# A two-layer fp32 block on one core: the opening loads and norms x first, and the context's rows are turned and normed beside the third and fourth query panel

## The reference, cut to what matters

```python
mod   = silu(c) @ ada_w + ada_b            # 1024 x 6144; shift1, scale1 are its first 2048 columns
mod_c = silu(c_ctx) @ ada_w + ada_b
h  = modulate(rms_norm(x,   norm1_w), sh1,  sc1)
hc = modulate(rms_norm(ctx, norm1_w), sh1c, sc1c)
q = h @ w_in[:, 0:512]                      # q is wanted for x alone
k, v, dt, xbc                               # are wanted for x and for the context
```

## Time and profile before

| | |
|---|---|
| runs | 2733.73, 2733.86, 2742.72 us; median 2733.86 |
| span of the profiled execution | 2732.2 us, which lies 1.7 us under the median |
| PE busy | 2546.3 us, 93% of the span |
| DVE, ACT, POOL busy | 50%, 36%, 36% |
| first and last product of query panels 0 and 1 | about 34 and 59 us |
| query panel 2 and 3 | from 61.17 and 67.31 us |
| first key panel | from 73.85 us |

### The profile page before, as it was taken

The page is one execution under the profiler, slowest core; times in us unless marked ns, Lnnn a source line. Parts: engine busy times, 40 slices in busy tenths (PEclk is TensorE's granted clock), DMA queues, the critical chain, the costliest instruction groups (busy, mean ns, idle before and its releaser), DMA issues.

```text
span 2732.2 us, 45723 instructions
## 1 busy us (share of the span) xinstructions
PE 2546.3 (93%) x19794; PEld 2286.5 (84%) x19794; DVE 1369.3 (50%) x2057; ACT 973.2 (36%) x1565; POOL 985.7 (36%) x585
## 2 busy tenths in 40 slices
PE   7989978799999999999999999989998979999997
PEld 5877767678888888887999999988988968999997
DVE  4634455462635354444264554466654534727363
ACT  5234344232323444334433332354332224333232
POOL 1743344544444322222434444500002214445444
PEclk9999999999999999999999999999999988999998
DMA  9432120333332221111222332322111012233221
GB/s 248 121 94 63 53 70 24 92 96 97 93 93 87 68 55 47 40 47 40 78 62 85 89 90 85 87 59 70 40 33 36 17 32 59 85 92 87 87 87 60
DMA packets 379927, 201.33 MB, mean 74 GB/s; under 512 B 6464, under 2 KB 377152, under 8 KB 379728
## 3 DMA queue, kind: packets, MB, share of 16 engines
q1 hardware_dynamic: 379728, 198.42, 25.8%
HBM read 196.30 MB, written 2.10 MB: 73 GB/s over the span
## 4 chain that ended last, share of the span: by engine, by line
PE 57%; DVE 22%; ACT 11%; issue 4%; POOL 4%; DMA 1%; POOLq 0%; ACTq 0%; SPq 0%; DVEq 0%
PE ps L645 40%; DVE t_ffy L2829 7%; ACT t_wh L613 5%; DVE t_ffy L2832 2%; ACT t_ffy L2736 2%; DVE t_atq L2628 2%; POOL t_wl L623 1%; PE ps L2436 1%; DVE t_wl L623 1%; DVE t_ffy L2838 1%; PE ps L3061 1%; PE ps L2409 1%; PE ps L2375 1%; PE ps L3080 1%; PE ps L1090 1%
## 5 line engine op out<-in xcount | busy, mean ns | idle before, releaser
L623 POOL TENSOR_TENSOR t_wl<-t_raw,t_wh 128x1024 fp32r<-128x1024 f32 (+2 forms) x268 | 611.1, 2281 | 1030.1 <-ACT t_wh L613 1030.1
L613 ACT ACTIVATE t_wh<-t_raw 128x1024 fp32r<-128x1024 f32 (+2 forms) x323 | 327.7, 1015 | 605.8 <-PE ps L645 562.4
L645 PE MATMUL ps<-t_hh,t_wh 128*128 128x264 f32 (+2 forms) x2048 | 473.4, 310 | 14.4 <-DVE t_dcq L2562 3.6
L645 PE MATMUL ps<-t_hh,t_wl 128*128 128x264 f32 (+2 forms) x2048 | 449.4, 298 | 8.0 <-POOL t_wl L623 4.3
L645 PE MATMUL ps<-t_hl,t_wh 128*128 128x264 f32 (+2 forms) x2048 | 446.0, 299 | 0.0
L645 PEld LDWEIGHTS ps<-t_hh,t_wh 128*128 128x128 f32 x2048 | 323.7, 192 | 36.5 <-issue 17.6
L645 PEld LDWEIGHTS ps<-t_hh,t_wl 128*128 128x128 f32 x2048 | 324.0, 191 | 24.2 <-POOL t_wl L623 6.9
L645 PEld LDWEIGHTS ps<-t_hl,t_wh 128*128 128x128 f32 x2048 | 322.6, 191 | 9.1 <-issue 1.5
L645 PE MATMUL ps<-t_fhh,t_wh 128*128 128x264 f32 (+1 forms) x1040 | 280.9, 324 | 6.5 <-DVE t_fhl L1753 4.9
L645 PE MATMUL ps<-t_fhh,t_wl 128*128 128x264 f32 (+1 forms) x1040 | 281.5, 325 | 4.6 <-POOL t_wl L623 4.5
L2829 DVE SCALAR_TENSOR_TENSOR t_ffy<-t_ffp,t_vec,t_ffy 128x528 f32<-128x528 f32 x88 | 216.8, 2463 | 130.6 <-ACT t_ffy L2736 130.6
(11 more groups left out here) (558 smaller groups left out, 4351.3 us busy)
## 6 DMA issues: line engine op xcount, KB each, us to landing
t_raw<-in_up SPq DMA_DIRECT2D x44, 512.0 KB, 3.8
t_raw<-in_up2a SPq DMA_DIRECT2D x44, 512.0 KB, 3.9
t_raw<-in_up2b SPq DMA_DIRECT2D x44, 512.0 KB, 3.9
t_raw<-in_attn_in SPq DMA_DIRECT2D x33, 512.0 KB, 4.1
t_raw<-in_dn_in SPq DMA_DIRECT2D x33, 512.0 KB, 4.1
t_raw<-in_ada_w SPq DMA_DIRECT2D x32, 512.0 KB, 4.4
t_raw<-in_w_in SPq DMA_DIRECT2D x25, 512.0 KB, 4.4
t_raw<-in_down SPq DMA_DIRECT2D x16, 512.0 KB, 3.8
```

Of the source, the lines that this page charges most:

```text
L613: ac.activation(wh[slot_of[j]][:, 0:kc, :], raw[r % NRAW][:, 0:kc, :], ACT.Copy).then_inc(up("wh_cut", "cut", j), 1)
L623: eng.tensor_tensor(wl[slot_of[j]][:, 0:kc, :], raw[r % NRAW][:, 0:kc, :], wh[slot_of[j]][:, 0:kc, :].bitcast(F), SUB).then_inc(up(name, " ...
L645: ins = pe.matmul(ps[bank_of(j, i)][:, 0:tn], wt[slot][:, k, :], a[:, k, t0:t0 + tn], start=first, stop=last)
```

## The change

x's four tiles come first and then four `ada_w` panels instead of context, meta rows and three. Slots become 12, and the copies of x out of PSUM go to VectorE, the Squares stay on ScalarE. The dummy matmuls go. A Sqrt on a scratch value is put behind the Silu. The context's and the meta rows' loads stand behind the last `ada_w` panel in SP's queue. Their turns, in banks of the ring of four, and the roots of the context's norm come when query panel 2 is taken; its spread and the 8 `norm1` and 8 `low1` of the context come when query panel 3 is taken. The diff, cut to its core:

```diff
-                    w.wait_ge(s.squared, at("squared", "turn_x", 4 + r))
+                    w.wait_ge(s.squared, at("squared", "turn_x", 2 + r))
...
-        xin = [slot(qT, 0), slot(qT, 1), slot(kT, 2), slot(zs, 0), slot(zs, 1), slot(vT, 0), slot(vT, 1)]
-        room = [slot(vT, 2)] + [slot(xbc, i) for i in range(6)]
-        slots = room + xin
+        xin = [slot(qT, 0), slot(qT, 1), slot(kT, 2), slot(zs, 0), slot(vT, 0), slot(vT, 1), meta_in]
+        room = [slot(vT, 2)] + [slot(xbc, i) for i in range(6)] + [slot(zs, 1)]
+        slots = room + xin[0:4]
...
+        def put_turn(i, of):
+            put("turn_x", i, banks=2, of=of)
+            for h in range(2):
+                sig.mark(copied_by(i), "turn_x", i, str(h))     # scaled (DVE) for i < 4, else copied (ACT)
+            if i < 6:
+                sig.mark("squared", "turn_x", i)
...
-        for i in range(7):
-            put("turn_x", i, banks=2, of=8)
-            if i < 6:
-                sig.mark("squared", "turn_x", i)
+        for i in range(4):
+            put_turn(i, 8)
         load_to(1)
         put("ada_rest")
         put_roots(NORM_X)
-        put_roots(NORM_C)
         put("ada_mm", 0, banks=1)
         put("ada_mm", 1, banks=1)
-        put_busy(NORM_X, 0, 5)
         put("ada_set", 0, banks=1)
         put_spread(NORM_X)
-        put_spread(NORM_C)
...
             put("norm1", c, x) ...
-            if c:
-                put("low1", c - 1, "c")
-            norm1_of(c, "c")
             put("low1", c, "x")
...
-                for i, (src, n, _, _) in enumerate(comes):
-                    sp.dma_start(xin[i][0:n, :], src).then_inc(slot_in[7 + i], 16)
-                for i in range(3):
+                for i in range(4):
+                    come(i)
+                for i in range(4):
                     ada_panel(i)
...
             def ada_rest():
-                for i in range(3, 7):
+                for i in range(4, 8):
                     ada_panel(i)
-                for i in range(7):
-                    w.wait_ge(s.copied, at("copied", "turn_x", i, "1"))
-                    ada_panel(7 + i)
+                for i in range(4):
+                    w.wait_ge(s.squared, at("squared", "turn_x", i))
+                    w.wait_ge(s.scaled, at("scaled", "turn_x", i, "1"))
+                    ada_panel(8 + i)
             def ada_mm(i):
-                if i < 2:
+                if i < 4:
                     w.wait_ge(s.ada_mm, at("ada_mm", "ada_mm", i))
-                    ada_panel(14 + i)
+                    ada_panel(NSLOT + i)
+                if i == 3:
+                    for x in range(4, 7):
+                        come(x)
...
+        def then_q(j, m):
+            then_first(j, m)
+            if m == 2:
+                for i in (4, 5, 6):
+                    put_turn(i, 4)
+                put_roots(NORM_C)
+            if m == 3:
+                put_spread(NORM_C)
+                norm1_of(0, "c")
+                for c in range(KD):
+                    if c + 1 < KD:
+                        norm1_of(c + 1, "c")
+                    put("low1", c, "c")
+
-        gemm(("q",), then_first, feed=feed_first)
+        gemm(("q",), then_q, feed=feed_first)
```

More of the change, by code:

```diff
@@ L128, in program @@
         raw_in = [ctx.enter_context(nc.semaphore(f"raw_in{i}")) for i in range(NRAW)]
-        slot_in = [ctx.enter_context(nc.semaphore(f"slot_in{i}")) for i in range(14)]
+        slot_in = [ctx.enter_context(nc.semaphore(f"slot_in{i}")) for i in range(12)]
+        x_in = [ctx.enter_context(nc.semaphore(f"x_in{i}")) for i in range(7)]
         def sbt(stack, name, shape, dt=F):
@@ L669, in program @@
         hl = sbt(sa, "hl", [128, KD, S + CT], R)
+        with ExitStack() as st:
+            meta_in = sbt(st, "metain", [NM, D])
         for stage in ("q", "k", "v", "dt", "xbc", "z"):
@@ L693, in program @@
         SH1, SC1, G1, SH2, SC2, G2 = (8 * i for i in range(6))
[L694 removed]
+        NORM_X = root_of(S, ssq[:, 0:4], ("squared", "turn_x", 3), 1.0 / D, rstd[:, 0:S], sums=False)
         NORM_C = root_of(CT, ssq[:, 4:6], ("squared", "turn_x", 5), 1.0 / D, rstd[:, S:S + CT], sums=False)
         SIGNALS.update({
[L698 removed]
+            "turn_x": "turned/0 turned/1", "silu_c": "cs_ready",
             "ada_mm": "ada_mm copied", "ada_set": "turned mod_set",
@@ L702, in program, with copied_by @@
         })
+        def copied_by(i):
+            return "scaled" if i < 4 else "copied"
+        def put_turn(i, of):
[4 more added lines that the diff above has]
+                sig.mark("squared", "turn_x", i)
         put("begin")
         put("silu_c")
-        for i in range(7):
-            put("turn_x", i, banks=2, of=8)
-            if i < 6:
-                sig.mark("squared", "turn_x", i)
+        for i in range(4):
+            put_turn(i, 8)
         load_to(1)
@@ L741, in feed_first @@
             if c == KD:
-                put("low1", KD - 1, "c")
                 return
@@ L788, in turn_x @@
                 n = comes[i][1]
-                w.wait_ge(slot_in[7 + i], 16)
+                w.wait_ge(x_in[i], 16)
                 w.wait_ge(s.cst_in, 16)
@@ L796, in turn_x @@
                     ins.then_inc(up("turned", "turn_x", i, str(h)), 1)
-                    free[b] = [(s.copied, at("copied", "turn_x", i, str(h)))]
+                    free[b] = [(handles[copied_by(i)], at(copied_by(i), "turn_x", i, str(h)))]
             def ada_mm(i):
                 b, = bank("ada_mm", i)
-                x = slots[i % 14].rearrange("p (k n) -> p k n", k=KD)
+                x = slots[i % NSLOT].rearrange("p (k n) -> p k n", k=KD)
                 held(b)
-                w.wait_ge(slot_in[i % 14], 16 if i < 7 else 32)
+                w.wait_ge(slot_in[i % NSLOT], 16 if i < NSLOT else 32)
                 w.wait_ge(s.cs_ready, at("cs_ready", "silu_c"))
@@ L832, in turn_x @@
                 if i < 6:
[L833 to L836, removed]
+                    w.wait_ge(x_in[i], 16)
+                    if i < 4:
+                        spent = rows_of(raw[i % 2])
+                        if i >= 2:
+                            w.wait_ge(s.squared, at("squared", "turn_x", i - 2))
+                    else:
+                        spent = slots[2 + i]
+                        w.wait_ge(s.ada_mm, at("ada_mm", "ada_mm", 2 + i))
+                    ac.activation(spent, xin[i], ACT.Square,
                                   accum_out=ssq[:, i:i + 1]).then_inc(up("squared", "turn_x", i), 1)
+                if i < 4:
+                    return
                 for h, b in enumerate(bank("turn_x", i)):
@@ L849, in silu_c @@
                 ac.activation(cs32[:, :, 1], col("c_ctx", 0, 8), ACT.Silu).then_inc(up("cs_ready", "silu_c"), 1)
+                w.wait_ge(s.eps_set, 1)
+                ac.activation(warm[:, :], eps[:, :], ACT.Sqrt)
             def ada_mm(i):
@@ L872, in begin, with turn_x @@
                                  ADD).then_inc(up("scaled", "begin", "s"), 1)
+            def turn_x(i):
+                _, n, dst, t0 = comes[i]
+                if i >= 4:
+                    return
+                for h, b in enumerate(bank("turn_x", i)):
+                    w.wait_ge(s.turned, at("turned", "turn_x", i, str(h)))
+                    view = ps[b][:, 0:4 * n].rearrange("p (j n) -> p j n", j=4)
+                    dv.tensor_copy(dst[:, 4 * h:4 * h + 4, t0:t0 + n],
+                                   view).then_inc(up("scaled", "turn_x", i, str(h)), 1)
             def ada_set(i):
@@ L888, in norm1 @@
                     w.wait_ge(st.sem, st.n)
-                w.wait_ge(s.copied, at("copied", "turn_x", 6, "1"))
+                if x == "x":
+                    w.wait_ge(s.scaled, at("scaled", "turn_x", 3, "1"))
+                else:
+                    w.wait_ge(s.copied, at("copied", "turn_x", 5, "1"))
                 w.wait_ge(s.rstd_a, at("rstd_a", "spread", NORM_X if x == "x" else NORM_C))
@@ L908, in modset @@
                                  ADD).then_inc(up("mod_set", "modset", n), 1)
-            return {"begin": begin, "ada_set": ada_set, "norm1": norm1, "low1": low1, "modset": modset}
+            return {"begin": begin, "turn_x": turn_x, "ada_set": ada_set, "norm1": norm1, "low1": low1, "modset": modset}
         def front_gpsimd(po, w, st):
```

8 lines of the change are left out of this document (5 added, 3 removed).

## The result

The changed kernel takes 2750.36 us (median of 4 runs, 2746.79 to 2755.70) against 2735.86 for the kernel before (4 runs, 2733.73 to 2742.72). The ratio is 1.0045 with a 95% interval of 1.0029 to 1.0061, so it is slower by about half a per cent. The prediction was 2744.6; it was built on the median of the three runs of the kernel before that were known then, 2733.86, so 2.0 of the 5.8 us between it and the measured median lie in that base. The profiled execution has a span of 2746.9 us (before: 2732.2), with the mean granted clock at 0.967 (before: 0.971).

A forecast was written before the change was run, and what follows sets the result against it. PE, busy for 93% of the span, was taken to bound the kernel. The terms -6.2+6.9+5.3+1.0+3.7 = +10.7 us took the span from 2732.2 to 2742.9, and the median to 2744.6 us; range 2730 to 2753.

The forecast's parts named there:

- part 1: Opening: the last modulation panel lands earlier and the feed catches up with the DMAs, last modulation product at 43.3; -6.2 us.
- part 2: End of query panel 2 (T): added transposes and a stall for banks ScalarE must copy out delay panel 3; +6.9 us.
- part 5: Granted clock: each of the two new stalls is followed by half-rate matmuls, 1.85 us each; +3.7 us.
- part 3: End of query panel 3 (T3): key panel 0 waits for the context's halves behind rope 1 and a low half; +5.3 us.
- Part 4: Key panel 0: GpSimd runs beside six of the context's 16 half operations and slows VectorE; +1.0 us.
- has thus landed at about 46.1: Opening, before the change: last modulation panel landed when DMA traffic ended, so the feed ran 3.4 us behind the DMAs.
- so 0: Opening: the clock falls, but up to the third chunk PE has over 1 us a chunk to spare; cost 0.
- All that gates it (cut 4's load, the rope) moves up with part 1: End of query panel 2: panel 4's load and the rope come earlier with the opening, so times relative to T hold.
- (b): Key panel 0: GpSimd collides with all the context's halves, about +13 us on the forecast, 2757.9 us; 12%.
- (a): Not slower: the stalls of part 2 and part 3 don't arise, median 2730.0 us; 13%.
- (c): One stall only: part of key panel 0's wait hides or VectorE is quicker, no second clock fall; 2737.5 us; 10%.
- (d): Opening: without the dummy matmuls the clock stays low through the feed, six chunks lose 14 us, 2758 us; 4%.

The follow-up runs named there:

- run 3: Changed kernel with the spread of the context's norm and its 16 halves put ahead of the sixth chunk of query panel 3; 2742.88 us, ratio 1.0027.
- run 1: Changed kernel with dummy matmuls back in the opening, behind ada_set 2 and beside modulation products 4 and 5; 2752.17 us, ratio 1.0056.
- run 4: Changed kernel with 8 dummy matmuls ahead of the meta rows' turn and 8 ahead of the first key product; 2749.72 us, ratio 1.0046.
- run 11: As run 6, with the context's halves split: chunks 0 and 1 inside query panel 2, the rest inside panel 3; 2739.96 us, ratio 1.0007.
- run 8: The kernel before without its dummy matmuls, one part of the change alone; 2736.51 us, ratio 1.0004.
- run 2: Changed kernel with the meta rows' turn in banks 1 and 3 in place of the banks of turn 4; 2747.72 us, ratio 1.0042.
- run 9: Changed kernel with GpSimd's multiply and two folds of modulations 2, 3 and 4 left out; 2748.10 us, ratio 1.0039.
- run 10: As run 7, with GpSimd's multiply and two folds of modulations 2, 3 and 4 left out; 2733.81 us, ratio 0.9992.
- run 5: Changed kernel with the meta rows' turn in banks 1 and 3, context's spread and halves before query panel 3's last chunk; 2741.22 us, ratio 1.0019.
- run 6: As run 5, but turns and roots when query panel 0 is taken, halves ahead of the third chunk of panel 3; 2738.71 us, ratio 1.0015.
- run 7: As run 6, with the dummy matmuls of run 1 in the opening; 2740.06 us, ratio 1.0013.

## Why the prediction was right in its mechanism and short by a few us

The side, the two waits, their places and their releasers came as forecast. In numbers, to the end of key panel 0 (before 82.18, after 94.02):

| stretch | terms | predicted | measured |
|---|---|---|---|
| up to the rope behind panel 2 | part 1 | -6.2 | -5.7 |
| from there to panel 3 | part 2 | +6.9 | +7.5 |
| panel 3 itself | part 5 | +1.85 | +2.4 |
| from its end to the first key product | part 3 | +5.3 | +5.1 |
| key panel 0 | parts 4 and 5 | +2.85 | +2.5 |
| sum | | +10.7 | +11.8 |

(-5.7 is 60.59 less 66.28, the rope's start in both timelines; +7.5 is 69.12 - 60.59 less the old 67.31 - 66.28; +2.4 is 7.82 less 5.46; +5.1 is 83.16 - 76.94 less 1.08; +2.5 is 10.86 less 8.33.) From there on the two traces run in parallel, +12.0 at the dt point. So at the dt point the changed kernel is 1.3 us later than the sum of the terms had it, +12.0 against +10.7. The other 2.7 us of the span lie in the tail that scatters by more than this, and are not explained; nor is the extra distance between the medians, 14.5, from the 12.0 shown.

**Part 1, the opening: the sum was right by two errors.** Product 15 came at 45.58, not at 43.3: -3.9 in place of -6.2. The step that failed is "has thus landed at about 46.1": I read the end of the traffic as the landing of the last panel. The profile gives the landing itself. DMA issues of before that begin from 40.6 to 42.4 (count, KB each, us to landing):
```profile
t_xbc<-in_ada_w SPq DMA_DIRECT2D x1, 512.0 KB, 7.0
```
and of after, from 36.8 to 38.6:
```profile
t_xbc<-in_ada_w SPq DMA_DIRECT2D x2, 512.0 KB, 7.4
```
So it had landed at 40.70 + 7.0 = 47.7 before, and at about 36.9 + 7.4 = 44.3 after. Run 3's chain shows this edge: a DMA of 7.38 from 36.90 and product 15 right behind it, at 44.31. So before the change the feed was 1.8 us behind the DMAs and not 3.4. The load is 3.4 us earlier and the most that product 15 could gain is 5.2. The other step that failed is "so 0" for the clock of the feed. PE idled 4.3 us ahead of modulation product 4, the first of the feed, and the granted clock was 0.50 for the 13.6 us from 22.4. Timeline of PE, after:
```profile
23.90 1.08 PE L817 MATMUL ps<-t_xbc,t_raw 128*32 128x128 f32 x16 [4.32 <-DMA t_xbc<-in_ada_w]
```
and stretches of all engines, with columns as in the earlier trace rows:
```profile
34.00:36.00 2.00, 2.00 (x27) 1.50 (x30) 0.97 (x2) 0.84 (x2) 0.00 (x0) 0.50 1.18 289
36.00:38.00 2.00, 2.00 (x22) 1.43 (x12) 1.11 (x3) 0.32 (x2) 0.00 (x0) 0.98 1.20 291
```
The spare time of the first chunks did not cover that: 1.3 us were lost against the landing. Another 1.8 us came from what I had left unchanged, the low half of panel 2. It took 1.23 here and 2.92 before:
```profile
54.19 1.23 DVE L624 TENSOR_TENSOR t_wl<-t_raw,t_wh 128x1024 fp32r<-128x1024 f32 x1 [2.20 <-ACT t_wh L614]
```
PE waited about 0.1 us for it in place of 1.6. This is luck of timing and no property of the change. GpSimd's multiply of modulation 0 begins within 0.2 us of this low half in every trace, and whichever began first kept its time (VectorE where both began together). Here both began at 54.19; the low half took 1.23 and the multiply 2.99. Before, GpSimd began at 58.13 and VectorE at 58.19; the multiply took 1.90 and the low half 2.92. Runs 1, 4 and 11 are like the first case, the other seven of the changed order and run 8 like the second (runs 2 and 3: 2.83 and 2.87). And a part of the luck is paid back: the longer multiply holds back the load of panel 4 (part 2), and the first wait was 4.76 in after and 4.59 in run 1, but 3.62 and 3.97 in runs 3 and 9.

**Part 2** was mis-sized: panel 3 began at T+8.5 and not at T+7.7. (In the term +6.9, T+7.7 is counted from 66.3 and T+0.86 from 66.45; counted alike it is +6.7, against +7.5 measured.) "All that gates it (cut 4's load, the rope) moves up with part 1" failed for the load. Its raw buffer comes free with GpSimd's last fold of modulation 0, so it moved with GpSimd, by 3.8 us and not by 5.7: the issue came at 60.79 in place of 64.57, the cut at T+4.3 in place of T+3.3, and `take` ended at T+5.9 in place of T+4.8. Against this, Square 4 and the copies cost 1.7 and not 2.3, because turn 6 starts behind the first of the two copies. The wait came to 4.76 (predicted 4.5), and the meta transposes, which I had at 0.6, took 1.00. Run 2 shows the mechanism, since other banks remove the wait entirely.

**Part 5** was mis-sized in its first half: 2.15 by run 4, not 1.85. Run 9 gives the second half as 1.7 (10.06 less 8.33). The rule of the Trainium skill (TensorE: Matmul & The Clock Gate, HAM oscillation) is borne out in direction by both waits, with 0.50 behind 4.76 and behind 4.69 us. The wait ahead of 61.17, which the prediction took as 2 us, was 1.64.

**Part 3** was right: start at T3+6.2 against T3+6.4, since GpSimd was quiet there as supposed and the low half took 1.22. **Part 4** was right in size, 0.8 by run 9 against 1.0; a `norm1` and a `low1` collided, the rest ran alone. Timeline of VectorE, after:
```profile
85.80 2.01 DVE L926 SCALAR_TENSOR_TENSOR t_sqb<-t_kT,t_gain,t_rstd 128x256 f32<-128x256 f32 x1
87.72 1.51 DVE L933 SCALAR_TENSOR_TENSOR t_hl<-t_sqb,t_mod,t_hh 128x256 fp32r<-128x256 f32 x1
```
and of GpSimd, with its idle time ahead:
```profile
85.58 1.95 POOL L949 TENSOR_TENSOR t_raw<-t_raw,t_small 128x1024 f32<-128x1024 f32 x1 [7.91 <-DMA t_raw<-in_ada_w]
```
GpSimd had waited 7.91 us for its load, which is the gate that I had set against rival (b).

The Trainium skill's rule on the shared SBUF interfaces (GPSIMD Engine Reference, Key points) agrees with these rows: 2.01 and 1.51 beside GpSimd, 0.48 each without it.

**The rivals.** (a), no waits: fell, both are in the trace. (b), GpSimd on all halves: fell for this order, but run 2 shows how little it takes: with the first stall gone, GpSimd's work fell beside the rope. (c): fell, the clock fell twice. (d), the clock low all through the feed: half true. It was low for 13.6 us and cost 1.3 and not 14. It rose again at 36.1, and until then the chunks had only three products each, since panel 1 runs two chunks behind: such a chunk took 4.55 at half rate (29.56 to 34.11), not 5.9. The 5.9 was right for a chunk with six products: in run 2, where the clock rose at 41.1, one took 5.83.

**What the order costs.** Making the load of the last modulation panel land 3.4 us earlier could bring 5.2 us at most, and moving the context's work behind it cost at least the 2.3 us of transposes that had lain in idle time. With all waits of this stretch gone (run 10, which leaves work out) the dt point is 2.0 ahead of before; with the work done (run 11) it is 0.5 behind. Both are single traces, and openings of this kind differ by up to 3.6 us. Whether another place for the halves would win the last microsecond stays open.

## What to carry to other kernels

Work moved off a stretch bound by DMA lands in a dense one, where in-order queues make it cost more than its busy time: for each moved step, write down what stands ahead of it on its engine and which buffers (here the ring of four banks) its last instruction needs back. Place its first instruction a rope, a cut and a copy earlier than its user, not directly before it. Then look at what it pushes back in turn: in run 11 the early halves delayed a rope, and a PSUM bank came free late. And take the landing of a load from its own record, not from the time at which the traffic seems to end.

## What the runs showed of the hardware that I had not expected

- **The clock's recovery is not the same twice.** Behind the same idle time of some 4 us in the same opening code it stayed at 0.50 for about 10 us (run 3), 13.6 (after) and about 20 (runs 2 and 9), and product 15 came at 44.31, 45.58, 47.91 and 47.63. One trace of an opening of this kind can be 3.6 us off another. The landing of the last panel moves too: PE waited for it until 44.31 in run 3, 44.88 in run 5 and 45.72 in run 6.
- **A fall can follow a short gap.** Idle times of 1.28 and 1.49 us (run 11) and 1.6 (before, ahead of 61.17) left the clock at 1.00. In runs 4 and 6, idle times of 2.02 and 1.90 were followed by 0.50, although PE had been dense until then. In run 1 it fell at about 35, behind idle times of 0.93 and 0.78 in a stretch in which PE was busy about half of the time. Which of length and history decides, these runs do not tell.
- **GpSimd's price on VectorE** was up to some four and a half times the time alone: 0.48 alone and 2.01 (after) to 2.16 (run 7) for a `norm1` of 128x256, 1.22 alone and up to 2.96 (run 5) for a low half of 128x1024. Where the two began together it could also be GpSimd that paid: its multiply of 128x1024 took 1.90 or 2.99, by which engine was first.
